# One variance per token and head in the norm of a recurrent branch, and loads of the last mixing stage issued during the stage before it

## The reference, cut to what matters

```
# block 1, recurrent branch, 8 heads of 64
y = rwkv7_scan(r, decay, k, v, kk, a)                     # [T, 8, 64]
mu = mean(y, axis=-1); var = mean(square(y - mu), axis=-1)  # per token and head
y = (y - mu) * rsqrt(var + 64e-5) * gn_g + gn_b
y = (y + sum(r*k*r_k) * v) * silu(gate)
# block 1, sparse attention branch, 8 heads; each query block of 128 keeps its 256 best keys
# x1 = rmsnorm(x + concat(y_rwkv, y_attn) @ w_out)
# block 2: latent attention, 12 heads, then attention to the memory, 4 heads of 64, 256 keys
s = q_mem . k_mem / 8; p = softmax(s); mem_out = p @ v_mem
y2 = concat(attn, mem_out) * silu(gate)
out = rmsnorm(x1 + y2 @ w_out)
```

## Time and profile before

| | us |
|---|---|
| median of 3 runs | 4506.92 (4504.72 to 4507.43) |
| profiled execution | 4512.46 |
| its span | 4510.6 |

### The profile page before, as it was taken

How to read it: one execution, slowest core, us unless ns; L and a number is a source line. 1 busy time by engine, 2 the same in 40 slices (tenths; PEclk the granted TensorE clock), 3 DMA queues, 4 the chain that set the end, 5 groups by cost and what they waited for, 6 DMA issues and landing times. The chain is left out here.

```text
span 4510.6 us, 75715 instructions
## 1 busy us (share of the span) xinstructions
PE 3992.4 (89%) x30840; PEld 2784.7 (62%) x30840; DVE 2765.1 (61%) x5076; ACT 2174.5 (48%) x3171; POOL 1144.9 (25%) x919
## 2 busy tenths in 40 slices
PE   7999999758988888887669899797999999999879
PEld 5767767445656556655458687585555555555467
DVE  5556464557768788888565323244676777777433
ACT  4445354586788778787433323122333333333431
POOL 1111111135434343433101000000344444444100
PEclk9999999878989999898679899898999999999989
DMA  4334233311211211211056533465223232322143
GB/s 129 96 106 128 80 109 98 92 38 37 49 33 40 50 40 35 55 41 30 26 177 202 197 127 127 170 222 170 48 64 71 55 80 55 71 65 49 50 165 113
DMA packets 388091, 404.92 MB, mean 90 GB/s; under 512 B 115776, under 2 KB 287488, under 8 KB 387488
## 3 DMA queue, kind: packets, MB, share of 16 engines
q1 hardware_dynamic: 385648, 393.10, 30.3%
q10 hardware_dynamic: 2096, 6.99, 0.4%
HBM read 248.36 MB, written 151.62 MB: 89 GB/s over the span
## 5 line engine op out<-in xcount | busy, mean ns | idle before, releaser
L142 ACT ACTIVATE PT<-psum 128x1024 f32<-128x1024 f32 x384 | 394.2, 1027 | 699.0 <-PE psum L132 695.6
L170 DVE TENSOR_REDUCE m<-psum 128x1 f32<-128x1024 f32 x384 | 467.8, 1221 | 302.3 <-PE psum L132 302.3
L132 PE MATMUL psum<-xc,wah 128*128 128x512 f32 x1600 | 514.6, 403 | 3.2 <-DVE xc L146 2.9
L146 POOL TENSOR_TENSOR part<-PT 128x1024 f32<-128x1024 f32 x144 | 342.0, 2375 | 558.2 <-DVE all L146 381.9
L132 PE MATMUL psum<-PT,V 128*64 128x512 f32 x1536 | 370.3, 603 | 0.0
L143 ACT ACTIVATE bias<-score,cand,cols 128x2048 bf16<-128x2048 f32 (+6 forms) x217 | 314.4, 1449 | 100.9 <-DVE cand L158 97.2
L132 PEld LDWEIGHTS psum<-xc,wah 128*128 128x128 f32 x1600 | 299.7, 190 | 79.4 <-issue 10.3
L143 ACT ACTIVATE sgn<-score,cand,cols 128x1920 bf16<-128x1920 f32 (+6 forms) x217 | 291.1, 1342 | 118.9 <-DVE cand L158 114.4
L146 POOL TENSOR_TENSOR Lm<-gm,cst 64x512 f32<-64x512 f32 x192 | 258.9, 1348 | 302.8 <-PE psum L132 154.0
L132 PE MATMUL psum<-hc,w4h 128*128 128x512 f32 x1024 | 321.0, 395 | 11.3 <-ACT w4h L142 11.3
L132 PE MATMUL psum<-xc,wal 128*128 128x512 f32 x800 | 315.7, 395 | 0.0
(11 more groups left out here) (334 smaller groups left out, 8790.9 us busy)
## 6 DMA issues: line engine op xcount, KB each, us to landing
raw_a<-in_w_a SPq DMA_DIRECT2D x50, 512.0 KB, 4.0
raw_w<-in_w_in SPq DMA_DIRECT2D x32, 512.0 KB, 4.4
QNh<-scr_qnh SPq DMA_DIRECT2D x48, 256.0 KB, 5.2
QRh<-scr_qrh SPq DMA_DIRECT2D x96, 128.0 KB, 5.0
QNl<-scr_qnl SPq DMA_DIRECT2D x48, 256.0 KB, 6.9
xin<-in_x SPq DMA_DIRECT2D x16, 512.0 KB, 4.1
scr_AR<-AR SPq DMA_DIRECT2D x32, 256.0 KB, 2.2
scr_BK<-BK SPq DMA_DIRECT2D x32, 256.0 KB, 2.3
```

The lines of the kernel that those rows point to most:

```text
L132: return self.e.matmul(out, a, b, start=start, stop=stop, skip_group_check=True)
L142: return self.e.activation(out, src, f, bias=bias, scale=scale)
L146: return self.e.tensor_tensor(out, a, b, op) if self.e else self.vector(out)
L170: return self.e.tensor_reduce(out, a, AX, op, negate=negate) if self.e else self.vector(a)
```

## The change

In stage 1 the norm has three pieces. `gn1` now makes four matmuls with the squares as weights and two columns of `blk` as moving data: the result is [128 tokens, 8], one sum per token and head. DVE makes variance + 64e-5 of it (`iv`), POOL raises it to -1/2. `gn2` multiplies `iv`, broadcast along 64 columns, by the identity, which puts the factor back on the 64 rows of each head in bank 2 (8 matmuls); DVE multiplies `yc` by it. ACT's Sqrt, DVE's reciprocal and POOL's first product are no longer there.

In stage 5 `order_m` is merged into `order_5`: its first piece goes ahead of the last `sum`, the next two ahead of the last four `rc`. SP loads the first two `qmt` at `gat` of unit 23. At `m1` of n = 1 it waits for the last `pv` of the latent attention and loads `x[0]` and the 8 weight tiles of `mix2`; after the store of `mout` 5 it loads its first 3 `y` tiles. `Mix` lays these buffers first (top False) and its own code issues these loads no more.

```diff
@@ stage 1: weights of the planner's merge, pieces, bank 2
-                    "sc": 2.0, "gn0": 3.0, "gn1": 5.0, "kT": 0.9, "vv": 0.9}.get(what, 0.4)
+                    "sc": 2.0, "gn0": 3.0, "gn1": 2.0, "gn2": 4.0, "kT": 0.9, "vv": 0.9}.get(what, 0.4)
+        iv = sb("iv", [128, 8])
+        heads_of = blk.rearrange("p (a b) -> p a b", a=2)[:, :, 0]
-            return [k for k in out if k != ("yout", -1)] + [("gn0", i), ("gn1", i)]
+            return [k for k in out if k != ("yout", -1)] + [("gn0", i), ("gn1", i), ("gn2", i)]
-                b2 = {"lv0": (i_act, "xl"), "lvy": (i_act, "y"), "gn0": (s_dve, "yc"), "gn1": (s_act, "gn")}[k[0]] + k[1:]
+                b2 = {"lv0": (i_act, "xl"), "lvy": (i_act, "y"), "gn0": (s_dve, "yc"), "gn1": (s_dve, "gv"),
+                      "gn2": (s_dve, "yn")}[k[0]] + k[1:]
@@ pe_2
+                    elif what == "gn1":
+                        q.wait_ge(s_act, "y2", i)
+                        for h in range(4):
+                            t = q.mm(bank[2][:, 2 * h:2 * h + 2], y2[:, h, :], heads_of)
+                        t.then_inc(*s_pe.up("gn1", i))
                     else:
-                        q.wait_ge(s_act, "y2", i)
-                        q.mm(bank[2], blk, y2[:, :, :]).then_inc(*s_pe.up("gn1", i))
+                        q.wait_ge(s_pool, "iv", i)
+                        for h in range(4):
+                            for e in range(2):
+                                t = q.mm(bank[2][64 * e:64 * e + 64, 128 * h:128 * h + 128],
+                                         iv[:, 2 * h + e:2 * h + e + 1].broadcast_to([128, 64]), ident)
+                        t.then_inc(*s_pe.up("gn2", i))
@@ act_2
-                    q.act(y2[:, :, :], quads(bank[2]), ACT.Sqrt, bias=epg[:, :], scale=1.0 / 64).then_inc(*s_act.up("gn", i))
@@ dve_2
-                    q.recip(y2[:, :, :], y2[:, :, :]).then_inc(*s_dve.up("iv", i))
+                    q.wait_ge(s_pe, "gn1", i)
+                    q.wait_ge(s_pe, "gn2", i - 1)
+                    q.ts(iv[:, :], bank[2][:, 0:8], 1.0 / 64, 64e-5, ALU.mult, ALU.add).then_inc(*s_dve.up("gv", i))
+                elif what == "gn2":
+                    q.wait_ge(s_pe, "gn2", i)
+                    q.wait_ge(s_dve, "yc", i)
+                    q.tt(yc[:, :, :], yc[:, :, :], quads(bank[2]), ALU.mult).then_inc(*s_dve.up("yn", i))
@@ pool_2
-                    q.tt(yc[:, :, :], yc[:, :, :], y2[:, :, :], ALU.mult).then_inc(*s_pool.up("yn", i))
+                    q.tt(iv[:, :], iv[:, :], neghalf[:, 0:8], ALU.pow).then_inc(*s_pool.up("iv", i))
+                elif what == "gn2":
+                    q.wait_ge(s_dve, "yn", i)
@@ Mix: for the last stage the row buffers come first (with a pad), then wh, wl, yh, yl
@@ mix_sp, mix_act: with top False no loads of the weights, of y for i < 3, of x for i == 0
@@ stage 5
+        done = order_5.index(("acc", NST - 1)) + 1
+        end_5 = order_5[done:]
+        order_5 = order_5[:done] + order_m[:1] + end_5[:1] + order_m[1:3] + end_5[1:]
+        order_5 += order_m[3:]
@@ sp_5, piece gat
+                    if u == NUN - 1:
+                        for m in range(2):
+                            q.dma(qmt[m][:, :], feat("qm")[:, 0, 512 * m:512 * m + 512]).then_inc(*d_qm[m].up(m))
@@ sp_5, piece m1
+                    if k[1] == 1:
+                        q.wait_ge(q_pe, "pv", NST // 2 - 1, 1)
+                        q.dma(mix2.x[0][:, :], mix2.resid[0:128, :]).then_inc(*mix2.d_r[0].up(0))
+                        for c in range(8):
+                            q.dma(mix2.raw[c][:, :], mix2.weight[c]).then_inc(*mix2.d_w[c].up(c))
-                    q.wait_ge(q_dve, "y", NUN - 1)
+                    q.wait_ge(q_dve, "y", NUN - 2 + m if m < 2 else NUN - 1)
@@ sp_5, piece mout
+                    if m == 5:
+                        q.wait_ge(d_y5[0], "m", 4)
+                        for i in range(3):
+                            q.dma(mix2.y[i][:, :, :], feat("y2T")[:, :, 128 * i:128 * i + 128]).then_inc(*mix2.d_y[i].up(i))
```

More of the change, by code:

```diff
@@ L1147, in program @@
         for k in rwkv_order:
-            if k[0] in ("lv0", "lvy", "gn0", "gn1"):
+            if k[0] in ("lv0", "lvy", "gn0", "gn1", "gn2"):
                 b2_free[k] = b2
-                b2 = {"lv0": (i_act, "xl"), "lvy": (i_act, "y"), "gn0": (s_dve, "yc"), "gn1": (s_act, "gn")}[k[0]] + k[1:]
+                b2 = {"lv0": (i_act, "xl"), "lvy": (i_act, "y"), "gn0": (s_dve, "yc"), "gn1": (s_dve, "gv"),
+                      "gn2": (s_dve, "yn")}[k[0]] + k[1:]
         pvs = {k[1:]: n for n, k in enumerate(k for k in dsa_order if k[0] == "pv")}
@@ L1171, in lane_2 @@
             return {"ld": "inverse", "gram": "inverse", "lv0": "inverse", "lvy": "inverse", "lvl": "inverse", "lvu": "inverse", "gn0": "norm",
-                    "gn1": "norm", "yout": "norm", "kT": "kv", "vv": "kv", "qd": "scores", "score": "scores", "exp": "scores", "pT": "values",
+                    "gn1": "norm", "gn2": "norm", "yout": "norm", "kT": "kv", "vv": "kv", "qd": "scores", "score": "scores", "exp": "scores", "pT": "values",
                     "pv": "values", "rb": "values", "fin": "values"}.get(what, "chunks")
@@ L1355, in pe_2 @@
                     t.then_inc(*s_pe.up("y", i, c))
-                elif what in ("gn0", "gn1"):
+                elif what in ("gn0", "gn1", "gn2"):
                     i = k[1]
@@ L1717, in pool_2 @@
                 what = k[0]
-                if what in ("gn1", "log", "nobias", "eq", "tie"):
+                if what in ("gn1", "gn2", "log", "nobias", "eq", "tie"):
                     q.wait_ge(i_pool, "lm", *halves)
@@ L1798, in __init__, with rows @@
                 self.source, self.weight, self.resid, self.gain = source, weight, resid, gain
+                def rows():
+                    self.y = two(f"{name}_y", [128, 8, 128], n=3)
+                    self.x = two(f"{name}_r", [128, D], n=3)
+                    self.o = two(f"{name}_o", [128, D], n=3)
+                    self.g = two(f"{name}_q", [128, D], n=3)
+                    self.raw = self.o + self.g + self.x[1:3]
+                if not top:
+                    rows()
+                    self.gf = sb(f"{name}_g", [128, D])
+                    self.pad = sb(f"{name}_pad", [128, D])
                 self.wh = sb(f"{name}_wh", [128, 8, D], FR)
@@ L1802, in __init__ @@
                 self.yl = two(f"{name}_yl", [128, 8, 128], FR)
[L1803 to L1807, removed]
+                if top:
+                    self.gf = sb(f"{name}_g", [128, D])
+                    rows()
                 self.junk = sb(f"{name}_j", [128, D], BF16)
                 self.ss = sb(f"{name}_ss", [128, 3 * NT])
-                self.raw = self.o + self.g + self.x[1:3]
                 if top:
@@ L1858, in mix_sp @@
                     c = k[1]
-                    if c % 2 == 0:
+                    if c % 2 == 0 and M.top:
                         q.dma(M.raw[c][:, :], M.weight[c]).then_inc(*M.d_w[c].up(c))
@@ L1862, in mix_sp @@
                     i = k[1]
+                    if i < 3 and not M.top:
+                        continue
                     q.wait_ge(M.dve, "yl", i - 3)
@@ L1866, in mix_sp @@
                     i = k[1]
+                    if i == 0 and not M.top:
+                        continue
                     if i in (1, 2):
@@ L1935, in mix_act @@
                 q.dma(M.g2[:, :], A["g_row2"]).then_inc(*M.d_g2.up())
-            for c in range(1, 8, 2):
+            for c in range(1, 8, 2) if M.top else ():
                 q.dma(M.raw[c][:, :], M.weight[c]).then_inc(*M.d_w[c].up(c))
@@ L2694, in columns @@
             return slice(1024 * (u % 2) + 512 * w, 1024 * (u % 2) + 512 * w + 512)
+        mix2 = Mix("m2", "y2T", A["w_out2"], scratch["x1"], A["final_g2"], False)
+        done = order_5.index(("acc", NST - 1)) + 1
+        end_5 = order_5[done:]
+        assert [k[0] for k in end_5] == ["sum"] + ["rc"] * 4 + ["out"]
+        order_5 = order_5[:done] + order_m[:1] + end_5[:1] + order_m[1:3] + end_5[1:]
+        order_5 += order_m[3:]
         def sp_5(q):
@@ L2726, in sp_5 @@
                               y5[u % 2][64 * w:64 * w + 64, :, :]).then_inc(*d_y5[u % 2].up(u, w))
-            for k in order_m:
-                if k[0] == "m1" and k[1] % 4 == 0:
+                elif k[0] == "m1":
+                    if k[1] == 1:
[3 more added lines that the diff above has]
+                            q.dma(mix2.raw[c][:, :], mix2.weight[c]).then_inc(*mix2.d_w[c].up(c))
+                    if k[1] % 4:
+                        continue
                     m = k[1] // 4
@@ L2826, in pe_5 @@
                     t.then_inc(*q_pe.up("sum", u))
-            for k in order_m:
-                what = k[0]
-                if what == "m1":
+                elif what == "m1":
                     n = k[1]
@@ L2894, in act_5 @@
                     t.then_inc(*e_act.up("exp", n))
-                elif what == "m2":
```

(1 more changed line is left out.)

18 lines of the change are left out of this document (6 added, 12 removed).

## The result

| kernel | runs | median us (all runs) | ratio to before, 95% |
|---|---|---|---|
| before | 4 | 4507.18 (4504.72 to 4510.25) | |
| after | 4 | 4439.89 (4437.14 to 4444.66) | 0.9852 (0.9834 to 0.9869) |

A forecast was written before the change was run, and what follows sets the result against it. No engine fills stage 1, where PE waits for DVE and ACT; later PE waits for `qmt` and weights. Stages 5 and 6 gain 17 us, stage 1 6, together 23: 4484 us predicted, range 4455 to 4508.

The forecast's parts named there:

- Order and early `qmt`: Stage 5, joint after memory attention: PE's wait for `qmt` goes, n = 4 starts earlier; 9.5 us gained, 5 to 10.5.
- Early `y`: Stage 5 end: three `y` loads ahead of the last `qmt` on SP's queue make PE wait; 5 us lost, 3 to 9.
- Stage 6: Start of stage 6: with data already loaded, PE's long run starts at 13.4 us, not 25.8; 12.4 us gained, 10 to 15.
- PE's added work: Stage 1: new `gn1` and `gn2` matmuls add 20.2 us of PE, of which 81%, 16.4 us, counts; 4 to 40.
- the prediction's signs: Expected in the profile after, stage 1: one table load, DVE busy 39 us less, PE about 20 more, `iv` wait under 10.
- The wait for POOL's `iv`: Stage 1: `gn2` stands in PE's queue for POOL's power, which the planner reckons too short; 5 us lost, up to 36.
- Relief: Stage 1: time freed on DVE (2.46 us per norm) and ACT (2.93), at share 0.32; 27.5 us gained, 9 to 43.
- all queues of the stage are ordered anew: Stage 1: changed merge weights give every queue a new order, worth plus or minus 10 us.
- Rival A: Stage 1: relief of DVE and ACT is worth more, PE's new matmuls fall into gaps; 4463 us, chance 0.20.
- B: Stage 1: PE stands behind `gn2` for the power, 45 us; stage loses 34 us, whole 4524; chance 0.13.
- D: Stages 5 and 6: preloads do not take hold, only stage 1's 6 us remain; 4501, chance 0.17 shared with C.
- C: Stage 1 gives nothing, `y` loads hold PE 9 us, new order 6 worse; 4500, chance 0.17 shared with D.

The follow-up runs named there:

- b_only: New loads and order of stages 5 and 6 alone, old norm, against the kernel before: 4491.73 us, ratio 0.9964.
- experiment 4: Changed kernel with the 8 `gn2` matmuls issued three times per norm, hidden from the planner: 4448.52 us, 0.9875 to before; stage 1 8.4 us longer than after.
- w333: `y_late` with the norm's three merge weights set to 3.0 each, only stage 1's order changed: 4430.40 us, 0.9831 to before; stage 1 1386.5 us.
- before_w9: Kernel before with `gn1`'s merge weight 6.0 instead of 5.0, another order of the old norm: 4499.99 us, 0.9988 to before; stage 1 1440.5 us.
- Experiment 5: Changed kernel with five plain ACT copies of `y2` per norm, no table load, hidden from the planner: 4487.14 us, 0.9958 to before; stage 1 52.8 us longer.
- w8: Changed kernel with `gn2`'s merge weight 3.0 instead of 4.0, only stage 1's order changed: 4460.63 us, 0.9902 to before; stage 1 1405.9 us.
- experiment 8: Planner merge weights changed in kernels with new and old norm, same instructions: stage 1 1386.0 to 1411.4 us (new), 1424.8 to 1444.0 us (old).
- y_late: Changed kernel with the three early `y` loads issued behind the last `qmt`: 4434.84 us, 0.9841 to before; again 4429.25 against 4436.14 for after.
- w10: `y_late` with `gn2`'s merge weight 5.0, only stage 1's order changed: 4449.03 us, 0.9871 to before; stage 1 1411.4 us.
- both_back: Changed kernel executing Sqrt and reciprocal again, results unused, with the planner reckoning with both: 4474.34 us, 0.9927 to before; stage 1 1423.3 us.

## Why the prediction was wrong

**Stages 5 and 6 were right.** Forecast 17, read from rows 8.0 - 6.6 + 12.7 = 14; `b_only` as a whole is 14 us faster (10 to 22 by its interval). Order and early `qmt`: 8.0 for 9.5, within the ends of 5 and 10.5; missed was the half clock behind the wait for `y`, so n = 4 starts 6.0 us after `out` and not 4. The new loads were hidden, as said. Early `y`: 6.6 lost for 5; the step left out that the wait brings the clock down and so lengthens what follows by 2.3. Stage 6: 12.7 for 12.4.

**The step that failed is stage 1: "27.5 - 16.4 - 5 = 6 us gained"; measured 57.** No single term accounts for it. In size:

- *PE's added work "20.2 us in 16 norms; PE is busy for 81% of the stage, so 16.4 us of it count".* The work is (1.14 + 1.13 - 1.13) x 16 = 18 us, near 20.2. The weight is wrong: a dose on PE costs 0.30 (experiment 4; 0.7 at most), so 5 us. PE's busy time did not rise by 20 us, as the prediction's signs have it, but fell by 4, since the clock went from 0.88 to 0.90. A busy share is not the share of added time that counts; with 0.81 for the busiest engine and 0.32 for the others I had ranked them by how full they are, and the doses, read from the traces, rank them the other way. 11 us.
- *The wait for POOL's `iv`, 5.* PE did not wait for it, although the power took 1.67 us, three times the row I took. By the prediction's own rule (price less the planner's 0.27) this price gives 22 us, so the step is wrong, and that 5 is no farther off is luck: in 15 of 16 groups the planner's order leaves 4 us or more behind the power. 5 us.
- *Relief, "a share of 0.32. I apply it to both engines", 27.5.* In a fixed order the doses give 0.65 (DVE) and 0.79 (ACT), with part of the queue moved 0.57 (both), in one refitted order 0.39. On the 42.9 and 47.5 us that the two engines lost that is 65, 52 or 35 us: 8 to 38 more than forecast. The method read what PE lacks in the 8 us behind a reciprocal's start. It counts a delay only where it first shows and by one window's length. That the delay is handed on, through the queues of DVE and ACT to the pieces behind, would explain the gap, and it fits that PE's waits for the attention's `pt` and the inverse's `Xl` fell most; the path itself is argued, no run shows it. Nor does any run part it from bank 2, for whose three shorter holds the prediction had -3 to +3.
- *"all queues of the stage are ordered anew: plus or minus 10 us".* Weights alone make 19 and 25. The mean over orders with the new norm is 41 us under that with the old. So about 41 of the 57 are the norm's (relief of some 46 less 5 for PE), and about 16 are that before had the longest of its three orders and after nearly the shortest of its five. With three and five orders, `w333` close to after and before within 4 us of `before_w9`, these means are good to perhaps 10 us.

By these the stage adds up as 46 - 5 - 0 + 16 = 57, where relief and order were fitted to that sum and only the 5 and the 0 were measured by themselves. Rival A named the mechanism, relief worth more and PE's matmuls in its gaps, but gave it 21 us more, where 51 were missing, since it kept the share of 0.32 nearly as it was. B (PE behind `gn2`) and D (the preloads do not take hold) are refuted by the idle time ahead of `gn2`, 0.0 us, and the rows of stage 6. C's mechanisms are halfway there: the `y` loads did cost 6.6, the stage did not give nothing.

**Of the drain.** The Trainium skill (ScalarE: Activation LUTs, "What ACT_TABLE_LOAD costs") gives a switch a drain besides the load. The row had none, and the trace decides: 12 ns behind 27 of the 29 loads before. Experiment 5 agrees with it: ACT with table loads is no dearer than ACT busy as long without.

**What stays open.** What in an order makes 20 us, but for `w8` and its wait for `wu`: between the ends of experiment 8 the clock moves by 0.02 and 0.01 and PE's busy time by a few us, and no single wait holds it. Also whether ACT's dose really counts for more than DVE's.

## What to carry to other kernels

Where several engines are each 75 to 80% busy and hand blocks to one another, price an edit by a dose: put the operation back, or in twice, hidden from the planner, compare the two traces' orders (a wait can move the queues even where the operation is hidden), and read the stage; neither busy share nor the local dip behind an operation gives its price (0.81 and 0.32 assumed, 0.30 and 0.65 to 0.8 found, each from one trace). Where queues are ordered by a planner, time three or four orders of both kernels before a difference of 20 us is given to the edit. A small load that someone waits for goes ahead of large ones on its queue, even when the large ones are meant for later.

## What the runs showed of the hardware

- POOL's power on 128x8 takes 1.67 us, on 128x1 0.56: some 0.16 us for each element more by these two sizes.
- The issue of a DMA can itself stand: 2.99 us on SP for a `qmt` of 256 KB behind three loads of 512 KB, 0.43 us for the same load where they come later (`y_late`).
- An ACT table load of 1283 ns had no idle time to speak of around it: 17 to 19 ns ahead, 12 ns behind wherever the next instruction's input was there (27 of 29 before).
- A wait of 6.61 us of PE cost 2.3 us more in what followed: the window of 14.66 us behind it had a granted clock of 0.82, that of 11.34 us behind a wait of 1.85 us in `y_late` had 1.00.
- The busy times of ACT and DVE together are 1.47 to 1.52 times the length of stage 1 in all kernels of this case (before 2155.2 / 1444.0 = 1.49, after 2064.8 / 1386.6 = 1.49, `w10` 1.47, `both_back` 1.52). It describes the traces; it is no law.
